# Strassen's seven products for the output projection of a hybrid attention and retention layer, from the second row block on

## The reference

```
h    = rms_norm(x) * norm_gain
proj = h @ w_in                        # 1024 -> 5632 columns: aq ak av ag rq rk rv rg
attn = windowed attention of aq, ak, av (16 heads of 64, 4 key/value heads, chunks of 64,
       QK-norm, ALiBi, one learned sink per head)
ret  = retention of rq, rk, rv (8 heads, 64 x 128 state), GroupNorm per head, * ret_norm_gain
out  = x + concat(attn * silu(ag), ret * silu(rg)) @ w_out      # 2048 -> 1024 columns
```

## Time and profile before

| what | us |
|---|---|
| median of 3 runs (1573.39 to 1574.0) | 1573.85 |
| span of the profiled execution | 1571.6 |
| TensorE (PE) busy in it | 1552.0 |
| VectorE (DVE) busy | 1124.6 |
| ScalarE (ACT) busy | 833.3 |
| GpSimd (POOL) busy | 457.9 |

### The profile page before, as it was taken

One profiled execution on the slowest core, in us unless ns is written; L12 is line 12 of the kernel. 1 busy time (PEld: TensorE's weight loads), 2 busy tenths in 40 slices (PEclk: granted clock), 3 DMA queues, 4 the chain that ended last, 5 costly groups with the idle time before them and its releaser, 6 DMA issues.

```text
span 1571.6 us, 24771 instructions
## 1 busy us (share of the span) xinstructions
PE 1552.0 (99%) x8120; PEld 1355.1 (86%) x8120; DVE 1124.6 (72%) x2874; ACT 833.3 (53%) x2331; POOL 457.9 (29%) x453
## 2 busy tenths in 40 slices
PE   6999999999999999999999999999999999999999
PEld 5898888988889888898988989889898898988887
DVE  7899587797856757577875766757687574775864
ACT  6766565655535445464654645446464454635641
POOL 6565657553322021120302212121120211202210
PEclk9999999999999999999999999999999999999999
DMA  8888485755775444463655635526447455344451
GB/s 319 308 287 310 155 334 215 269 210 212 296 258 197 161 177 183 165 236 125 215 206 208 250 140 186 211 97 249 172 158 281 146 207 191 140 191 137 174 212 54
DMA packets 123327, 323.65 MB, mean 206 GB/s; under 512 B 16832, under 2 KB 60224, under 8 KB 123200
## 3 DMA queue, kind: packets, MB, share of 16 engines
q1 hardware_dynamic: 122240, 320.50, 55.6%
q10 hardware_dynamic: 960, 1.57, 0.3%
HBM read 250.72 MB, written 71.30 MB: 205 GB/s over the span
## 4 chain that ended last, share of the span: by engine, by line
PE 92%; DVE 4%; POOL 1%; DMA 1%; issue 1%; ACT 1%; SPq 0%; DVEq 0%; ACTq 0%; POOLq 0%
PE jb L1469 26%; PE jb L1470 26%; PE jb L1471 26%; PE ob L1528 2%; PE s L1504 2%; PE ptb L1513 2%; PE ob L1488 1%; PE s L1567 1%; PE ab L1578 1%; PE s L1566 1%; POOL wL L396 1%; PE s L1405 1%; DMA stage<-wp_dram 1%; PE ab L1405 0%; PE ab L1407 0%
## 5 line engine op out<-in xcount | busy, mean ns | idle before, releaser
L1469 PE MATMUL jb<-wH,hTH 128*128 128x512 f32 (+1 forms) x1024 | 376.3, 367 | 13.0 <-POOL wL L396 10.7
L1470 PE MATMUL jb<-wL,hTH 128*128 128x512 f32 (+1 forms) x1024 | 372.6, 364 | 0.0
L1471 PE MATMUL jb<-wH,hTL 128*128 128x512 f32 (+1 forms) x1024 | 372.3, 364 | 0.0
L1469 PEld LDWEIGHTS jb<-wH,hTH 128*128 128x128 f32 x1024 | 193.0, 188 | 33.6 <-POOL wL L396 12.4
L1471 PEld LDWEIGHTS jb<-wH,hTL 128*128 128x128 f32 x1024 | 193.1, 189 | 20.4
L1470 PEld LDWEIGHTS jb<-wL,hTH 128*128 128x128 f32 x1024 | 193.3, 189 | 17.9
L1469 PE MATMUL jb<-wH,mxH 128*128 128x512 f32 x512 | 207.1, 405 | 0.9 <-ACT rawqn L550 0.6
L1469 PE MATMUL jb<-hTH,wH 128*128 128x512 f32 x512 | 201.4, 393 | 0.0
L1471 PE MATMUL jb<-wH,mxL 128*128 128x512 f32 x512 | 200.6, 392 | 0.0
L1470 PE MATMUL jb<-wL,mxH 128*128 128x512 f32 x512 | 200.5, 392 | 0.0
L1470 PE MATMUL jb<-hTL,wH 128*128 128x512 f32 x512 | 200.0, 391 | 0.0
(11 more groups left out here) (145 smaller groups left out, 3011.6 us busy)
## 6 DMA issues: line engine op xcount, KB each, us to landing
wH<-scrH SPq DMA_DIRECT2D x144, 512.0 KB, 7.0
wL<-scrL SPq DMA_DIRECT2D x144, 512.0 KB, 7.9
stage<-wp_dram SPq DMA_DIRECT2D x48, 512.0 KB, 6.7
scrH<-wH SPq DMA_DIRECT2D x48, 512.0 KB, 6.9
scrL<-wL SPq DMA_DIRECT2D x48, 512.0 KB, 7.8
wH<-scrH SPq DMA_DIRECT2D x48, 384.0 KB, 5.4
wL<-scrL SPq DMA_DIRECT2D x48, 384.0 KB, 6.6
out_dram<-acc SPq DMA_DIRECT2D x16, 512.0 KB, 3.0
```

The lines of the kernel that those rows point to most:

```text
L1469: pe.matmul(o, lh, rh_, start=i == 0, stop=False)
L1470: pe.matmul(o, lh, rl_, start=False, stop=False)
L1471: m = pe.matmul(o, ll, rh_, start=False, stop=i == last)
```

## The change

It leaves the projections and the attention and retention as they are and changes how the output projection is computed and how its weights are made and kept.

- **Units 4 to 15 (row blocks 1 to 3):** the 512 x 512 by 512 x 1024 product is taken as 2 x 2 blocks and formed from seven block products (Winograd's form of Strassen's scheme) in 14 jobs of 2 x 3 matmuls, in place of 8 jobs of 4 x 3. Four operand sums of the mixed values are made on GpSimd (`s3a`, `s2a`, `s4a`) and VectorE (in `mtl`) and split by ScalarE (`sh`) and GpSimd (`s1l` to `s4l`). Three of the products carry on in the PSUM bank of an earlier one (`CARRIED`). The output is kept in `acc` as differences, which GpSimd forms on loading (`ini`) and undoes at the end of a block (`fin`; in the last one VectorE, `fiz`).
- **Units 0 to 3** keep the 8 output jobs, now tiles in an inner loop and halves in the outer one.
- **Seven weight blocks** in place of four double subtiles: in units 4 to 7 their sums are made on VectorE (`wtw`), the high parts on ScalarE (`who`), the low parts on VectorE (`wld`, six) and GpSimd (`wlo`, one), and saved; units 8 to 15 reload them.
- **Raw weights of units 0 to 3:** five of eight low parts of the Q, G and V panels, and four of eight of the output panel, are made on VectorE instead of GpSimd.
- **The retention gain** goes into the rows of `w_out` (`scale`, and the scale in `wh1`); `ggm` and its transfer are gone.
- **Weight buffers** are a ring of 7 slots of one chunk (2 subtiles, 1024 columns) in place of 2 panels of 4 chunks; a chunk's slot comes free during the last job that reads it (`s_rel`).
- **Queues:** stores and reloads of `acc` move from SP to ScalarE's queue, in quarters; `xl` of row blocks 1 to 3 moves from VectorE to GpSimd.
- **Order:** output jobs lie in pairs between the Q and G jobs of the next unit; all orders are rewritten.

```diff
-J_QKV, J_AG, J_RQ, J_RK, J_RVG, J_OUT, JOBS = 0, 4, 6, 7, 8, 12, 20
+J_QKV, J_AG, J_RQ, J_RK, J_RVG, J_OUT, JOBS = 0, 4, 6, 7, 8, 12, 26
+W_CHUNKS = [4, 4, 4, 7]
+SLOTS = 7
+RING = SLOTS * 1024
+MADE = 2 * NU
+STACKED = MADE + 1
...
+OUT_JOBS = [(i_, p_) for i_ in (1, 2, 5, 4, 7, 3, 6) for p_ in range(2)]
+EIGHT = "Q0 Q1 Q2 a0 Q3 a1 a2 a3 b0 b1 G0 b2 b3 G1 G2 G3 V0 V1 V2 V3".split()
+FIRST = "Q0 Q1 Q2 10 11 Q3 20 21 G0 50 51 G1 40 41 G2 70 71 G3 30 31 60 61 V0 V1 V2 V3".split()
+TURN = FIRST
+WOVEN = "Q0 Q1 10 11 Q2 20 21 Q3 50 51 G0 40 41 G1 70 71 G2 30 31 G3 60 61 V0 V1 V2 V3".split()
+CARRIED = {2: 1, 4: 5, 3: 7}
+OPERAND = {1: 0, 2: 1, 4: 2, 5: 0, 6: 3, 7: 4, 3: 1}
...
+LOW_ON_DVE = [1, 2, 3, 4, 5, 6]
+GAINED = [2, 3, 6, 7]
+WL_ON_DVE = [1, 2, 4, 5, 7]
...
+            def s2a(n):
+                pool.wait_ge(S["s_s1a"], nth(n - NU, 2, 1))
+                pool.wait_ge(S["s_mixl"], mixed(n, 1))
+                pool.wait_ge(S["s_s3a"], n - NU + 1)
+                pool.tensor_tensor(flat(mix0[:, :, :, :]), flat(mix1[:, :, :, :]), flat(mix0[:, :, :, :]), ALU.subtract
+                                   ).then_inc(S["s_s2a"], 1)
...
+            def s1l(n):
+                pool.wait_ge(S["s_s1h"], n - NU + 1)
+                pool.tensor_tensor(flat(mxL[:, 0]), flat(mix1[:, :, :, :]), flat(mxH[:, 0]).bitcast(F32), ALU.subtract
+                                   ).then_inc(S["s_s1l"], 1)
...
             def mtl(n, t):
+                turned = ab[:, 0:256].rearrange("p (h q) -> p h q", h=2)
                 v.wait_ge(S["s_mth"], nth(n, 4, t))
-                sub(mxL[:, 2:4, t * P:(t + 1) * P], ab[:, 0:256].rearrange("p (h q) -> p h q", h=2),
-                    mxH[:, 2:4, t * P:(t + 1) * P]).then_inc(S["s_mtl"], 1)
+                if t >= 2 and n >= NU:
+                    v.wait_ge(S["s_s3a"], n - NU + 1)
+                    v.tensor_tensor(mix1[:, t - 2], mix1[:, t - 2], turned, ALU.add).then_inc(S["s_s1a"], 1)
+                sub(mxL[:, 1 + t // 2, t % 2], turned, mxH[:, 1 + t // 2, t % 2]).then_inc(S["s_mtl"], 1)
...
+            def wtw(n, i):
...
+                if i == 0:
...
+                    v.tensor_tensor(t1, b12, b11, ALU.subtract).then_inc(S["s_twin"], 1)
...
+            def wld(n, c):
+                out_low(v, n, c).then_inc(S["s_old"], 1)
...
-                    pe.wait_ge(S["s_acc"], nth(m, 8, k - J_OUT))
+                    pe.wait_ge(S["s_acc"], ADD_DONE[m, k])
...
+                    prod, half = product_of(j)
+                    chunk = chunk_of(n, j, 0)
...
+                    at = OPERAND[prod]
                     o = bank_of(n, j)[:, :]
-                    pairs = [((mxH[:, k, cols], mxL[:, k, cols]), (W[:, 4 * h + k, :], L[:, 4 * h + k, :]))
-                             for k in range(4)]
-                    first = t == 0
+                    pairs = [((mxH[:, at, half, k], mxL[:, at, half, k]), (hi(chunk)[:, k], lo(chunk)[:, k])) for k in range(2)]
+                    first, begins = half == 0, prod not in CARRIED
...
-            job(9, 0); I(8, 2); MT(8, 0); job(9, 1); job(9, 2); I(8, 3); TQ(9, 0); MT(8, 1); job(9, 3)
...
+            I(8, 3); TQ(9, 0); MT(8, 1); job(8, 12); job(8, 13); job(9, 2); MT(8, 2); S_(9, 0); TQ(9, 1); job(8, 14)
+            job(8, 15); MT(8, 3); job(9, 3); S_(9, 1); job(8, 16); job(8, 17); PT(9, 0); job(9, 4); TQ(9, 2); PT(9, 1)
```

More of the change, by code:

```diff
@@ new lines, in tile_out, with mixed, last_use, ring_places @@
+def tile_out(n, t):
+    return max(JOB_DONE[n, J_OUT + 4 * h + t] for h in range(2))
+def mixed(n, t):
+    return 4 * n + t + 1 if n < NU else 4 * NU + 2 * (n - NU) + t + 1
+def last_use(chunk):
+    n, p, c = chunk
+    if p == 3:
+        return last_out(n, c)
+    return JOB_DONE[n, (J_AG, J_RVG, J_OUT)[p] - 1] - (3 - c) / 4
+def ring_places():
+    free, places = [0] * SLOTS, []
+    for n, p, c in CHUNKS:
+        size = 2 * W_WIDTH[p]
+        if p == 0 and c:
+            places.append((places[-1][1], places[-1][1] + size))
+        elif p == 0:
+            at = min(range(SLOTS - 2), key=lambda i: (max(free[i:i + 3]), i))
+            free[at:at + 3] = [last_use((n, p, 3))] * 3
+            places.append((1024 * at, 1024 * at + size))
+        else:
+            at = min(range(SLOTS), key=lambda i: (free[i], i))
+            free[at] = last_use((n, p, c))
+            places.append((1024 * at, 1024 * at + size))
+    return places
@@ new lines, with released @@
+EARLY_AT = {k: i for i, k in enumerate(EARLY)}
+def released(chunk):
+    n, p, c = chunk
+    if p == 3:
+        return "s_job", last_out(n, c)
+    if c < 3:
+        return "s_rel", EARLY_AT[chunk] + 1
+    return "s_job", JOB_DONE[n, PANEL_LAST[p]]
+PLAIN = [k for k in CHUNKS if k[0] < NU]
+PLAIN_AT = {k: i for i, k in enumerate(PLAIN)}
+RAW = [k for k in CHUNKS if k[0] < NU or k[0] < MADE and k[1] == 3 and k[2] in (1, 6)]
+RAW_AT = {k: i for i, k in enumerate(RAW)}
+OUT_ORDER = {u_: [c_ for n_, p_, c_ in CHUNKS if n_ == u_ and p_ == 3] for u_ in range(NU, MADE)}
@@ new lines, in place_free, with stage_done @@
+        def place_free(engine, chunk):
+            waits = {}
+            for old in before_in_ring(chunk):
+                name, value = released(old)
+                waits[name] = max(waits.get(name, 0), value)
+            for name, value in waits.items():
+                engine.wait_ge(S[name], value)
+            for old in before_in_ring(chunk):
+                if old in SAVE_AT:
+                    engine.wait_ge(*saved(old))
+        def stage_done(engine):
+            engine.wait_ge(S["s_twin"], 4 * NU)
+            for c in (3, 4, 5):
+                engine.wait_ge(S[low_done(MADE - 1, c)[0]], low_done(MADE - 1, c)[1])
@@ L528, in _ @@
+            s4a(15); s4l(15)
         @block.scalar
@@ L1472, in job @@
+                    pe.matmul(o, lh, rh_, start=begins and i == 0, stop=False, **go_on)
+                    pe.matmul(o, lh, rl_, start=False, stop=False, **go_on)
+                    m = pe.matmul(o, ll, rh_, start=False, stop=i == last, **go_on)
+                    if j in PANEL_LAST and i % 2 == 1 and i < last:
+                        m.then_inc(S["s_rel"], 1)
                 m.then_inc(S["s_job"], 1)
```

1629 lines of the change are left out of this document (934 added, 695 removed).

## The result

The changed kernel takes **1625.3 us** (1622.4 to 1630.0), the kernel before 1573.6 beside it: ratio 1.0333, 95% interval 1.0321 to 1.0345. That is 52 us slower; I had forecast 26 us faster, and the result lies above my whole range of 1538 to 1565. The profiled execution has a span of 1620.2 us against 1571.6.

A forecast was written before the change was run, and what follows sets the result against it. TensorE was taken as the bound: span 1571.6 - 32.6 + 5.2 + 2.4 - 1.5 + 0.7 = 1545.8 us, and with the median 2.25 us above the span, 1548.0 us; range 1538 to 1565.

The forecast's parts named there:

- Part 1: Output projection in 12 units: seven products save 144 matmuls at 0.2267 us, -32.6 us; other matmuls and transposes stay.
- Part 2: VectorE's added work in units 4 to 15: stalls of +5.2 us in units 4 to 7, +2.4 in the others.
- 0.34 us of VectorE per us of GpSimd: Price of the two engines disturbing each other, taken at its upper bound from the profile's windows; lower bound nothing.
- Part 3: Units 0 to 3: low parts moved to VectorE, earlier start; -1.5 us, bounds -5 to +5.
- the signs that I had named: Forecast is wrong if units 8 to 15 take over 97 us, or the first 392 us lose more than before.
- Part 4: The end: a subtraction joins the addition after the last product, +0.7 us.
- Part 5: Transfers: reloaded weights in 7 slots and acc transfers in ScalarE's queue, priced at 0; bounds 11 us and 3 us.
- Rival D: Three PSUM banks emptied late at 7 places per unit, 4.8 us per unit, up to 1598 us; chance 0.10.
- A: Rival: nothing stalls, the order hides all the added work, 1540.4 us; chance 0.15.
- B: Rival: VectorE bounds units 4 to 7 as weight operations stretch beside GpSimd, 1560 to 1565 us; chance 0.18.
- C: Rival: operand sums come late for product 5 in units 9 to 15, 19 us, 1567; chance 0.07.

The follow-up runs named there:

- e13: Kernel before, with 71 of the 128 low parts of the weights of units 0 to 3 made on VectorE instead of GpSimd; 1572.3 us, ratio 0.9991.
- e17: Kernel before, with the last unit's first output job put ahead of the last Q job in units 1 to 14; 1601.3 us, ratio 1.0180.
- e18: Same job swap as e17 in the kernel before, with the engines' lists reordered to fit it; 1573.9 us, ratio 1.0003.
- e6: Changed kernel with most columns of acc additions, weight sums, low parts and operand sums left out in units 4 to 15, order kept; 1604.9 us, ratio 1.0202.
- e14: Changed kernel with all four lists reordered by a replay that includes VectorE-GpSimd meetings, plus the cuts of e6; 1589.5 us, ratio 1.0108.
- e10: Kernel before, with 80 GpSimd operations that nobody waits for added in units 6 to 15: subtractions 1576.3 us, powers instead 1573.9 us.
- e3: Changed kernel with three of four weight sums and low parts of four of seven weight blocks in units 4 to 7 cut to 16 columns; 1621.1 us.
- e4: Changed kernel with most GpSimd operations on the operand sums cut to 16 columns in units 4 to 15; 1613.3 us, ratio 1.0252.
- e19: The kernel of e13 with its four lists reordered by a replay of its own durations; 1573.8 us, ratio 1.0001.

## Why the prediction was wrong, point by point

- **Part 1, the matmuls: nearly right.** 1392 output matmuls are counted, 144 fewer. But "The other matmuls and transposes stay" was wrong: all matmuls fell only by 112 (8120 to 8008), since `STACKED` is 9 instead of 5 and units 5 to 8 form the retention groups with one matmul more each, 32 of some 0.1 us, 3 us. The saving shows where there are few stalls: unit 11 took 95.1 us with 2.6 us of stalls, before 96.3 with 0.9.
- **Part 2, VectorE: the failed step.** "An engine that works in order at 76% hid everything before (unit 7 was at 75 us without a stall); one at 91 to 99% does not." The forecast of VectorE's busy time was fair in sum, with the work one unit later than I had it: units 4 to 8 took 67, 92, 83, 83 and 86 us, 411 in all, where I had 86.5 three times, 94.4 and 72.6, 427 in all. What failed is reading the cover from it. Unit 1 grew by 13.8 us with VectorE 75% full (86.3 of 115.8), and in e13 it did not grow at 83%; unit 13, at 67 of 100.1 us, has a stall of 4.6. What hides work in an in-order list is how far each call stands ahead of its use in the other engines' order, and that was earned by the old order of jobs, not by the share (e17 and e18). I priced new stalls at 7.6 us; they measured 62.7, and the lower clock made them 74. Nor is it the load that carries most of it: e6 took the added work out and won 20 of 52 us, orders won up to 22, both together (e14) 36.
- **0.34 us of VectorE per us of GpSimd: the size was of the right kind, the meaning wrong.** e10 measured 50.3 us for about 102, 0.49, for subtractions, and nothing for powers. It is no even tax: single operations become up to 1.1 us longer in e10, small ones that others wait for too.
- **Part 3: the low parts were right, the bound was not.** The low parts alone gave -1.2 us. "TensorE was busy throughout from 196 us, so nothing is to be won there" took the old order for granted; with the new one units 1 to 4 lost 23.4 us. The first matmul stayed at 9.9 us, not 8.7. Of the signs that I had named, both came: unit 8 took 104.3 us and unit 13 100.1, over 97, and units 0 to 3 took 395.6 us against 374.8.
- **Part 4, the end: small, and smaller than said.** From the end of the last matmul to the end of the span are 4.0 us, before 3.8, where I had 0.7 more.
- **Part 5, transfers: right by TensorE's waits.** 2.7 us of waits for reloaded chunks, within the 11 us of its bound; 206 to 257 GB/s in the windows from 490 to 1470 us. But transfers are 5% of the chain, before 1%, and ScalarE waited 11.8 us for the raw weights `wraw`, a wait that the kernel before does not have. Whether that made other results late was not tested.
- **Rival D was on the right side, for another place.** In the changed kernel TensorE hardly waits for a bank to be emptied: VectorE's additions and ScalarE's read-outs had been moved in time. In e17, where they had not, this very mechanism cost 28 us, 2 us a unit, where I had priced 4.8. A had no support. B's mechanism did not come: its weight operations would have taken 2.47 us each, and the 24 low parts took 1.3 (`L401`, mean), though TensorE waits 6.9 us for them. C's late operand sums are not what the waits name; e3 and e4 show that weights and operand sums cost 4 and 12 us.
- **Still open:** some 40 us between e14 (1589.5) and my 1548. They lie mostly in units 1, 4, 5, 8 and 13, the lower clock in them included. That the job order of the changed kernel leaves too little distance at these places fits e17 and the timeline of unit 1, but no run gave it another job order: that is argued, not shown. That fixed lists out of step with the jobs can cost this much is shown in the kernel before (e17, e18).

## What to carry to other kernels

A busy share tells how much work an engine has, not whether it hides: with engines that work through a fixed list, measure for each result the distance between where it stands in its list and where it is used, and count a new order of the heavy engine's jobs as a change to every other list. One swap of two jobs cost 28 us with no work added, and moving the calls to match gave all of it back. Keep GpSimd's two-operand arithmetic away from short VectorE operations that another engine waits for, or give it work that does not hold VectorE up (here, powers).

## What the hardware did that I had not expected

- **TensorE's clock falls after a stall.** The kernel before had a granted clock of 1.00 in every window. In the changed kernel TensorE went to the lower level, 1.2 GHz, in six stretches of 3.4 to 6.8 us between its matmuls, each begun during a stall of 2.2 to 4.6 us or within 1.2 us of its end; the profile's window over one of them, after a stall of 3.16 us:

```profile
120.00:130.00 10.00, 5.81 (x23) 4.43 (x21) 8.79 (x23) 6.05 (x17) 2.40 (x3) 0.83 0.62 197
```

  They cost 11.7 us, a fifth on top of the 62.7 us of new stalls. Not each such stall brought a drop: those of 2.3 us at 243 us and of 3.1 us at 543 us did not (granted clock 1.00 in 200 to 300 and 500 to 600 us), nor did a wait of 1.2 us for `wL<-scrL`.
- **VectorE waits for the whole of a GpSimd operation**, and GpSimd for VectorE: in the changed kernel GpSimd's 1.29 us subtractions took up to 2.3 us where they began beside a long VectorE operation without PSUM operand. The 80 powers of e10 held nobody up.
- **An early start can be worth nothing**: in e19 TensorE began 1.6 us sooner, stood twice for 2.5 us soon after, and had a granted clock of 0.51 from 16 to 26 us, where the kernel before had 1.00.
